# Decode values of a paged attention: four samples on GpSimd with a buffer and load requests of its own, four on TensorE

## The reference

```python
k_past = cache_k[l][page_table].reshape(b_s, n_past, FOX_H, FOX_HD)   # 8 samples x 1024 x 4 x 128
v_past = cache_v[l][page_table].reshape(b_s, n_past, FOX_H, FOX_HD)
...
p = jax.nn.softmax(jnp.concatenate([s_past, s_new], axis=-1), axis=-1)
o = einsum('bhqk,bkhd->bqhd', p[..., :P], v_past) + einsum('bhqk,bkhd->bqhd', p[..., P:], v)
```

## Time and profile before

| | |
|---|---|
| median of 3 runs | 1726.88 us (1726.18 to 1727.52) |
| the profiled execution | 1725.65 us |
| its span | 1723.9 us |
| TensorE busy | 1699.3 us (99%) |
| VectorE busy | 1077.7 us (63%) |
| ScalarE busy | 798.8 us (46%) |
| GpSimd busy | 142.4 us (8%) |

### The profile page before, as it was taken

One profiled execution on the slowest core, in us unless ns is written; L12 is line 12 of the kernel. 1 busy time (PEld: TensorE's weight loads), 2 busy tenths in 40 slices (PEclk: granted clock), 3 DMA queues, 4 the chain that ended last, 5 costly groups with the idle time before them and its releaser, 6 DMA issues.

```text
span 1723.9 us, 33330 instructions
## 1 busy us (share of the span) xinstructions
PE 1699.3 (99%) x13788; PEld 1648.4 (96%) x13788; DVE 1077.7 (63%) x1263; ACT 798.8 (46%) x895; POOL 142.4 (8%) x148
## 2 busy tenths in 40 slices
PE   9999999999999999999999999999999999999995
PEld 8999888899999999999999999999999999999995
DVE  7888787756557666455587784444444444454655
ACT  5654544556544444444454554444444444333433
POOL 8200000000012555000000000000000000000000
PEclk9999999999999999999999999999999999999998
DMA  8565567776657877666555556555555555555651
GB/s 263 150 209 159 148 203 245 225 235 209 213 153 238 282 252 250 189 179 183 179 176 183 173 170 192 178 180 181 182 179 178 180 182 182 181 178 169 194 175 73
DMA packets 309126, 329.75 MB, mean 191 GB/s; under 512 B 12175, under 2 KB 289939, under 8 KB 308756
## 3 DMA queue, kind: packets, MB, share of 16 engines
q1 hardware_dynamic: 307612, 326.59, 61.7%
q10 hardware_dynamic: 1400, 1.54, 0.2%
HBM read 322.31 MB, written 5.77 MB: 190 GB/s over the span
## 4 chain that ended last, share of the span: by engine, by line
PE 96%; DVE 2%; DMA 1%; issue 0%; ACT 0%; ACTq 0%; SPq 0%; DVEq 0%
PE ps L778 15%; PE ps L779 15%; PE ps L1155 15%; PE ps L1156 15%; PE ps L780 15%; PE ps L1154 15%; PE ps L848 1%; PE ps L1027 1%; DMA w_in_ring<-in_w_in 1%; PE ps L827 0%; PE ps L883 0%; PE ps L816 0%; PE ps L801 0%; DVE w_split L1624 0%; PE ps L794 0%
## 5 line engine op out<-in xcount | busy, mean ns | idle before, releaser
L2310 DVE TENSOR_TENSOR w_lo<-w_raw,w_hi 128x1024 fp32r<-128x1024 f32 x264 | 322.8, 1225 | 326.0 <-ACT w_hi L1512 323.0
L1624 DVE TENSOR_TENSOR w_split<-w_in_ring,w_split 128x1024 fp32r<-128x1024 f32 x276 | 352.6, 1283 | 238.7 <-ACT w_split L1216 229.0
L778 PE MATMUL ps<-xh,w_split 128*128 128x264 f32 x1680 | 482.2, 287 | 1.7 <-DVE w_split L1624 1.7
L1512 ACT ACTIVATE w_hi<-w_raw 128x1024 fp32r<-128x1024 f32 x264 | 279.4, 1060 | 440.0 <-PE ps L1156 435.2
L779 PE MATMUL ps<-xl,w_split 128*128 128x264 f32 x1680 | 478.2, 285 | 0.0
L780 PE MATMUL ps<-xh,w_split 128*128 128x264 f32 x1680 | 476.7, 284 | 0.0
L1216 ACT ACTIVATE w_split<-w_in_ring 128x1024 fp32r<-128x1024 f32 x276 | 291.1, 1059 | 361.7 <-DMA w_in_ring<-in_w_in 268.1
L778 PEld LDWEIGHTS ps<-xh,w_split 128*128 128x128 f32 x1680 | 316.0, 188 | 20.2 <-issue 14.6
L1155 PE MATMUL ps<-x1l,w_hi 128*128 128x264 f32 x1152 | 327.8, 285 | 0.0
L1156 PE MATMUL ps<-x1h,w_lo 128*128 128x264 f32 x1152 | 327.0, 284 | 0.0
L1154 PE MATMUL ps<-x1h,w_hi 128*128 128x264 f32 x1152 | 326.0, 283 | 0.0
(11 more groups left out here) (473 smaller groups left out, 2138.8 us busy)
## 6 DMA issues: line engine op xcount, KB each, us to landing
w_in_ring<-in_w_in SPq DMA_DIRECT2D x210, 512.0 KB, 3.8
w_raw<-in_w_ffn_up SPq DMA_DIRECT2D x176, 512.0 KB, 3.5
w_raw<-in_w_ffn_down SPq DMA_DIRECT2D x88, 512.0 KB, 3.4
kv<-in_cache_k SPq DMA_DIRECT2D x64, 258.0 KB, 3.8
w_in_ring<-in_w_branch SPq DMA_DIRECT2D x32, 512.0 KB, 4.3
kv<-in_cache_v SPq DMA_DIRECT2D x64, 256.0 KB, 3.8
w_in_ring<-in_w_out SPq DMA_DIRECT2D x32, 512.0 KB, 3.4
x_t<-in_x SPq DMA_DIRECT2D x8, 264.0 KB, 6.6
```

The source lines that it names most:

```text
L778: nc.tensor.matmul(out, w_split[:, slot, 0, c], right_h[:, k, :], start=first, stop=False)
L1512: A_(w_hi[:, n % RING2, :], raw[:, n % RING2, :], ACT.Copy).then_inc(sem("hi2"), 1)
L1624: V.tensor_tensor(w_split[:, slot, 1, :], w_in_ring[:, slot, 1, :], w_split[:, slot, 0, :], ALU.subtract).then_inc(sem("lo_done"), 1)
L2310: V.tensor_tensor(w_lo[:, n % RING2, :], raw[:, n % RING2, :], w_hi[:, n % RING2, :], ALU.subtract).then_inc(sem("lo2"), 1)
```

## The change

GpSimd takes samples 0 to 3 whole (`V_POOL` = 4), and TensorE samples 4 to 7, in eight units at chunks `V_AT` = 155, 162, 168, ... 200. Buffer 0 of `kv` serves TensorE's units, loaded by SyncE; buffer 1 serves GpSimd. Its first four pages are loaded by SyncE behind chunk 154; for all later ones GpSimd loads the page number into a register and issues the DMA itself, for each page as soon as it has added it. GpSimd waits for each page by a semaphore of its own, and before it first writes the rows 2 and 3 of `v_sum` for the last chunk of branch 1. `v_add` is called once, ahead of TensorE's last unit, with four sums. The places of all other work stay.

```diff
-V_AT = [155 + 3 * u for u in range(16)]
-V_SCALED = [1, 3, 5, 7, 9, 11, 13]
+V_POOL = 4
+V_AT = [155, 162, 168, 175, 181, 188, 194, 200]
...
         def load_values(u, first):
-            if first == 0 and u < 2:
-                sp.wait_ge(sem("kv_used"), 16 + u - 1)
-                sp.wait_ge(sem("lf_taken"), 16 + u - 1)
-            elif first == 0 and u - 2 in V_SCALED:
-                sp.wait_ge(sem("v_scaled"), V_SCALED.index(u - 2) + 1)
-            elif first == 0:
-                sp.wait_ge(sem("kv_used"), 16 + len([v for v in range(u - 1) if v not in V_SCALED]))
-            pages("cache_v", u, first, u // 2, MIX)
+            if first == 0 and u == 0:
+                sp.wait_ge(sem("lf_taken"), 15)
+            if first == 0:
+                sp.wait_ge(sem("kv_used"), 16 + u if u else 15)
+            for j in (first, first + 1):
+                src = A["cache_v"][ds(page_register(8 * (V_POOL + u // 2) + 4 * (u % 2) + j), 1)].rearrange("o p c -> (o p) c")
+                sp.dma_start(kv[:, 0, j, 0:MIX], src).then_inc(sem("kv0"), 16)
+
+        def load_pool_values():
+
+            sp.wait_ge(sem("kv_used"), 16)
+            sp.wait_ge(sem("lf_taken"), 16)
+            for j in range(4):
+                src = A["cache_v"][ds(page_register(j), 1)].rearrange("o p c -> (o p) c")
+                sp.dma_start(kv[:, 1, j, 0:MIX], src).then_inc(sem("kv1"), 16)
...
+            if n == 154:
+                load_pool_values()
+            for u in range(8):
+                for first in (0, 2):
+                    if n == (V_AT[u - 1] + 6 if u else 152) + first // 2:
+                        load_values(u, first)
...
+        pool.wait_ge(sem("pt_loaded"), 16)
+        pool.wait_ge(*told("f_ptt", 1))
+        for u in range(2 * V_POOL):
+
+            b, half = u // 2, u % 2
+            out = v_sum[:, b, :]
+            if u == 4:
+
+                pool.wait_ge(*used(last_chunk(pass_of("branch", 1, 7))))
             for j in range(4):
-                at = 32 * (8 * b + 4 + j) + b
-                values = kv[:, u % 2, j, 0:MIX]
-                scaled = out if j == 0 else values
+                at = 32 * (8 * b + 4 * half + j) + b
+                values = kv[:, 1, j, 0:MIX]
+                first = half == 0 and j == 0
+                scaled = out if first else values
+                if u:
+                    pool.wait_ge(sem(f"kv_page{j}"), 16 * u)
+                elif j == 0:
+                    pool.wait_ge(sem("kv1"), 64 * 9)
                 then(pool.tensor_tensor(scaled.rearrange("p (h d) -> p h d", h=HEADS), values.rearrange("p (h d) -> p h d", h=HEADS),
                                         ptt[:, at:at + HEADS * DEC].rearrange("p (h m) -> p h m", m=DEC)[:, :, 0:1].to_broadcast([P, HEADS, P]),
                                         ALU.mult))
-                if j:
+                if not first:
                     then(pool.tensor_tensor(out, out, values, ALU.add))
-            pool.sem_inc(sem("v_scaled"), 1)
+                if u < 2 * V_POOL - 1:
+                    page = pool.value_load(pt[0:1, 4 * (u + 1) + j:4 * (u + 1) + j + 1], min_val=0, max_val=A["cache_v"].shape[0] - 1)
+                    pool.dma_start(values, A["cache_v"][ds(page, 1)].rearrange("o p c -> (o p) c")).then_inc(sem(f"kv_page{j}"), 16)
+        pool.sem_inc(sem("v_scaled"), 1)
...
+            b, half = V_POOL + u // 2, u % 2
             bank = claim(pe, "v_unit", 0)[0] if u == 0 else banks("v_unit", 0)[0]
-            if u == 8:
-                v_add(0, 4)
-            if u == 15:
-                v_add(4, 7)
-            pe.wait_ge(sem(f"kv{u % 2}"), 64 * (8 + u // 2 + 1))
+            if u == 7:
+                v_add()
+            pe.wait_ge(sem("kv0"), 64 * (8 + u + 1))
```

## The result

The changed kernel takes 1728.24 us (median of 20 runs, 1726.52 to 1729.61), beside 1725.35 for the kernel before in as many runs on the same chip (1724.11 to 1727.52). The ratio is 1.0013, with a 95% interval of 1.0007 to 1.0019. The difference of the medians is 2.9 us. The interval lies above 1: the change makes the kernel slower by about 0.1 to 0.2%, where 2.05 us faster was forecast. That is a small difference, within the 0.2% that the prediction would still have called the same, but on the wrong side of zero. The time lies in the range of 1723.2 to 1733. The forecast of 1724.8 was reckoned from 1726.88, the median of three runs; from 1725.35 it would have been 1723.3, so the sum is off by 4.9 us. The profiled execution took 1729.45 us, of which 1727.8 are its span.

The account below looks back on a forecast made before the run. TensorE's own instructions were taken to bound the kernel (96% of the chain); one unit (1.20) and three additions (0.85) fewer give 1725.65 - 2.05 = 1723.6, plus 1.23 for the median, 1724.8 us. Range: 1723.2 to 1733.

Parts of the forecast that it names:

- TensorE's part: On TensorE between chunks: one value unit (1.20 us) and three additions (0.85) fewer, 2.05 us less on the path.
- GpSimd's part: GpSimd's arithmetic 102.7 us plus 28 page loads 49.3, from 537.0 to 689.0, 7.0 us before TensorE needs the sum.
- GpSimd late: Rival, chance 0.27: page loads cost more than 1.76 us, TensorE waits ahead of its last unit; 1725 to 1751 us.
- SyncE and the loads: SyncE issues 36 value pages instead of 64, no longer waits for GpSimd (19.1 us before); nothing new waits, counted as nothing.
- Chunk 155: Four pages at chunk 154 delay chunk 155's weight load by some 2 us; 4.5 us of slack take it.
- VectorE, the term that turned the sign: GpSimd's added arithmetic delays VectorE's splits 3.2 us more over 150, hidden by VectorE's 49.6 us of waits nearly everywhere.
- the stall: TensorE's wait for VectorE's w_split at 581.72, kept at 1.15 us; that it goes or shrinks had chance 0.10.
- VectorE falls behind: Rival, chance 0.10: five more collisions with GpSimd in 551.4 to 568.6, stalls of 2 to 5 us, 1727 to 1730.
- requests held up by VectorE: Skill page's ground for the GpSimd late rival (0.27): GpSimd can't write DMA requests while VectorE is in two-port mode.

Follow-up runs that it names:

- e8: Kernel before the change, with fills in place of GpSimd's arithmetic: 1723.53 us, ratio 0.9984 to the kernel before.
- e6: Changed kernel with GpSimd's first pages in pairs behind chunks 146 and 147, and fills for its arithmetic: 1722.35 us, ratio 0.9983 to the kernel before.
- e4: Changed kernel with first pages in pairs behind chunks 146 and 147, and GpSimd pausing ahead of its eighth page until VectorE's cum_rows: 1722.1 us, ratio 0.9985.
- e3: Changed kernel without GpSimd's 28 page loads and their waits, working eight times on its first four pages: 1729.17 us, ratio 1.0024 to the kernel before.
- e2: Changed kernel with fills in place of GpSimd's multiplications and additions, page loads kept: 1722.56 us, ratio 0.9983 to the kernel before.
- e7: Changed kernel with first pages in pairs behind chunks 146 and 147, and GpSimd pausing ahead of its 17th page until chunk 178 is used: 1726.75 us, ratio 1.0003.
- e1: Changed kernel with GpSimd's first four pages loaded in two pairs behind chunks 146 and 147, not all behind chunk 154: 1726.4 us, ratio 1.0001.
- e5: Changed kernel with only GpSimd's pause ahead of its eighth page until VectorE's cum_rows: 1724.95 us, ratio 0.9993 to the kernel before.

## Why the prediction went wrong

The matmuls at both ends of the stretch give the account. These are the ends in the kernel before; then in the changed kernel; in e8; in e6 (TensorE's timelines):

```profile
546.07 1.07 PE L883 MATMUL ps<-kv,ptt 128*32 128x512 f32 x8
...
705.95 0.51 PE L893 MATMUL ps<-fold,v_part 128*128 128x8 f32 x4
```
```profile
546.37 1.07 PE L897 MATMUL ps<-kv,ptt 128*32 128x512 f32 x8
...
709.29 0.51 PE L907 MATMUL ps<-fold,v_part 128*128 128x8 f32 x4
```
```profile
546.23 0.64 PE L880 MATMUL ps<-kv,ptt 128*32 128x512 f32 x4
...
704.16 0.39 PE L890 MATMUL ps<-fold,v_part 128*128 128x8 f32 x3
```
```profile
546.19 0.64 PE L894 MATMUL ps<-kv,ptt 128*32 128x512 f32 x4
...
702.06 0.95 PE L904 MATMUL ps<-fold,v_part 128*128 128x8 f32 x8
```

| stretch, us | GpSimd's arithmetic | fills | lost to the arithmetic |
| --- | --- | --- | --- |
| before | 159.88 | 157.93 | 1.95 |
| changed | 162.92 | 155.87 (e6) | 7.05 |
| difference | +3.04 | -2.06 | +5.10 |

- **TensorE's part, right in the stretch.** A unit and three additions were put at 2.05 us; without collisions they are 2.06, by one trace each. e4 does the real work and has 155.87 too. Over the whole kernel no such gain is shown: e8 and e6 have ratios of 0.9984 and 0.9983.
- **GpSimd's part, right in the sum, partly by luck.** These are its third page load with the work on the page behind it, and its last addition, from its timeline in the changed kernel:

```profile
554.36 0.58 POOL L761 DMA_DIRECT2D kv<-in_cache_v  x1 [1.20 <-issue]
554.96 1.06 POOL L754 TENSOR_TENSOR kv<-kv,ptt 128x512 f32<-128x512 f32 x1
556.09 2.19 POOL L758 TENSOR_TENSOR v_sum<-v_sum,kv 128x512 f32<-128x512 f32 x1
...
685.17 2.15 POOL L758 TENSOR_TENSOR v_sum<-v_sum,kv 128x512 f32<-128x512 f32 x1
```

  A page costs 1.20 + 0.58 and the gap of 0.02, 1.80, beside 1.76 foreseen. The split was the other way about: the issue 0.58 where 1.05 was taken, the steps ahead of it 1.20 where SyncE's 0.71 was. GpSimd ends at 687.3 (689.0 foreseen), though it began at 540.90 and not at 537.0: it needed 146.4 us and not 152.0, and the two errors cancel. TensorE asks for the sum at 701.5, so 14 us lie between (6.7 in e4, where TensorE has no stalls). The rival with the largest chance, GpSimd late, fell; e3, in which it ends at 650, says the same from the other side.
- **SyncE and the loads, right but for one.** Its waits for GpSimd are gone, and no load of a value page made TensorE wait.
- **Chunk 155, the first step that failed.** It was said that the four pages hold its load back by some 2 us and that 4.5 us of slack take it. It went out at 532.9, 2.4 us later than before, and ScalarE split it 3.8 us later (539.02 against 535.21 before). What the step missed is that the split and ptt stand in line on ScalarE, and that VectorE's last two reciprocals of lnt stand behind the splits. VectorE's last reciprocal in the kernel before, and in the changed kernel:

```profile
542.36 1.79 DVE L2231 RECIPROCAL lnt<-lnt 128x264 f32<-128x264 f32 x1
```
```profile
546.79 1.79 DVE L2245 RECIPROCAL lnt<-lnt 128x264 f32<-128x264 f32 x1
```

  So VectorE went into its run of wide products 4.4 us late. Of these, 2.95 are the late load (chunk 155's split begins at 540.18 and not at 537.23). The other 1.5 are collisions with GpSimd, which starts at 540.90: two instructions between have their long forms, 1.55 for 0.70 and 2.00 for 1.37; in e2, with fills, the last reciprocal is back at 544.2. TensorE didn't feel chunk 155 itself; the slack that hid it was the slack that the next term needed.
- **VectorE, the term that turned the sign.** Its delay was scaled by GpSimd's busy time: 3.2 us more over 150, and the stall kept at 1.15. The rows say otherwise. Here are GpSimd's groups in 530 to 720 and then VectorE's splits in 540 to 700 of the changed kernel, beside the earlier trace rows:

```profile
L758 POOL TENSOR_TENSOR v_sum<-v_sum,kv 128x512 f32<-128x512 f32 x28 | 54.6, 1950 | 2.2
L754 POOL TENSOR_TENSOR kv<-kv,ptt 128x512 f32<-128x512 f32 x28 | 33.3, 1188 | 0.8
L761 POOL DMA_DIRECT2D kv<-in_cache_v x28 | 16.4, 585 | 34.5 <-issue 34.5
L754 POOL TENSOR_TENSOR v_sum<-kv,ptt 128x512 f32<-128x512 f32 x4 | 4.7, 1163 | 30.2 <-ACTq L245 30.1
```
```profile
L1638 DVE TENSOR_TENSOR w_split<-w_in_ring,w_split 128x1024 fp32r<-128x1024 f32 x48 | 80.0, 1681 | 35.9 <-ACT w_split L1230 33.8
```

  GpSimd's shortest multiplication is 1.05 and its shortest addition 1.28. Above these it lost (43.2 - 29.4) + (36.4 - 26.9) = 23.3 us before and (38.0 - 33.6) + (54.6 - 35.8) = 23.2 after: eleven more instructions, and no more delay. VectorE, against the busy time with fills, lost 108.25 - 87.94 = 20.3 before and 124.56 - 89.86 = 34.7 after. So all the new delay fell on VectorE, 14.4 us. The prediction reckoned with the splits alone: 3.2 us more, where they took 48 x (1.681 - 1.225) = 21.9 us beyond the short form, 8.0 more than before. The multiplications, now behind a page issue, got short (1.54 to 1.19); the additions got longer (1.74 to 1.95). That VectorE lost more is measured. The pause of the issue can be a part of the cause only: in e3, without issues, GpSimd loses (52.9 - 33.6) + (52.2 - 35.8) = 35.7 us, 12.5 more, and VectorE 120.6 - 89.9 = 30.7, 4 less, which is still 10 more than in the kernel before.

  The place was wrong too. It was said that bl and the split are in their long form already, so that the stall can hardly grow. VectorE's timeline in the changed kernel:

```profile
554.77 2.37 DVE L2249 TENSOR_TENSOR hf<-hf,lnt 128x1056 f32<-128x1056 f32 x1
...
562.30 2.18 DVE L1638 TENSOR_TENSOR w_split<-w_in_ring,w_split 128x1024 fp32r<-128x1024 f32 x1
...
585.43 2.25 DVE L2273 SCALAR_TENSOR_TENSOR cum_k<-cum,ident 4x1024 fp32r<-4x1024 f32 x1
```

  The first product ran in 1.25 us before and takes 2.37; the split at 562.30 ends at 564.48, and TensorE, waiting for it since 562.60, goes on at 564.62. The stall of 581.72 didn't grow where it was but shrank (0.41 at 583.97); two others opened on either side, 19 us ahead and 5 us behind. A long form at one place said nothing on its neighbours.
- **The rival "VectorE falls behind" named the mechanism** (collisions in 551 to 569, a slack of 4.5 us, 1727 to 1730) and got 0.10. What spoke for it, five more collisions against 4.5, was in the text; what was set against it was 2.24 us of idle time ahead of 568.28. The late chunk 155 takes 3 us from that same slack. Two terms drew on one account and each was checked against it alone; together, 2 to 3 and 5 against 4.5, they should have made it the likeliest case.
- **The clock wasn't in the sum.** 1.7 of the 5.1 us come from 3.4 us at 1.2 GHz. The traces with 3.4 us or more of waits in this stretch have such a drop at 589 or 590.5 (the changed kernel, e3, e7); those with at most 2.04 (before, e1, e2, e4, e5, e6, e8) have none there. But waits alone don't settle it. All ten traces have a single wait of 2.0 to 2.2 us for w_lo at 923 to 932; behind it the clock falls for 3.4 us in three of them (before, changed, e8) and not in the other seven. Here are the kernel before, then e4, the wait and the window behind it:

```profile
927.19 0.36 PE L1154 MATMUL ps<-zh,w_hi 128*128 128x266 f32 x1 [2.01 <-DVE w_lo L2310]
...
927.00:933.00 6.00, 5.81 (x35) 5.84 (x36) 5.57 (x10) 2.73 (x5) 0.00 (x0) 0.72 0.69 200
```
```profile
923.47 0.36 PE L1170 MATMUL ps<-zh,w_hi 128*128 128x266 f32 x1 [2.02 <-DVE w_lo L2326]
...
923.00:929.00 6.00, 5.53 (x44) 5.56 (x45) 5.57 (x10) 2.73 (x5) 0.00 (x0) 1.00 0.64 187
```

  Such drops are also most of what sets one execution apart from another. In the 66 executions of the kernel before that were timed beside the experiments, the mean granted clock was 0.996 in 22, 0.995 in 29 and 0.994 in 15, and their mean times are 1724.5, 1726.0 and 1727.5: steps of 1.5 us, about the price of one drop. So the 1.7 us in the stretch are what one traced execution lost; how often the changed kernel loses them there isn't known. The waits have 3.25 of the 5.1 us, 4.4 less 1.15. What is left, 7.05 - 4.4 - 1.7 = 1.0, no row names, but the kernel before has as much, 1.95 - 1.15 = 0.8, so it hardly enters the difference.
- **Outside the stretch,** the span grew by 3.9 us in all against 3.04 in it: 0.3 lies ahead of unit 0, 0.6 behind the fold. One part of that is plain: the wait for ml, 0.6 before and 1.1 after (0.9 to 1.4 in e1, e2 and e4 to e7). So a part of TensorE's gain is given back later: e8 and e6 are 2.06 apart in the stretch and 2.4 in their spans, but 1.7 of these are the drop of the clock that only e8 has at 926, and their ratios are the same within their intervals.
- **The range held by luck.** It was drawn wide for a GpSimd that is late; 1728.24 lies in it for another reason.

The section Who interferes with whom of the Trainium skill's page "SBUF — State Buffer" says that a VectorE instruction with two inputs in SBUF contends with a GpSimd instruction that reads SBUF and not with one that only writes. The runs agree: 1225 ns a split beside fills (e2), 1681 beside arithmetic. The rival that the same section suggested, requests held up by VectorE, wasn't seen: the 28 issues on GpSimd took 577 ns in the middle and 776 at most.

## What to carry to other kernels

Work moved from the bounding engine to an idle one is paid for by whoever shares a resource with the idle one; price it where the third engine's queue has the least slack, not over the stretch, and add up all terms that draw on the same slack before holding them against it. A measured mean of two engines' mutual delay need not scale with busy time: here GpSimd's share stayed and VectorE's grew by 70%, and without the issues the shares were different again. Where the spot is known, let the helper engine stand aside for just that long: 6.5 us of pause and an earlier load turned 0.13% slower into 0.15% faster, and GpSimd was still done 6.7 us ahead of need. And differences of 0.1% are of the size of one drop of the clock, so they want many runs, and the trace of more than one execution.

## What the runs showed of the hardware

- A page load issued by GpSimd with its page number from a register keeps GpSimd for 0.58 us, and 1.20 us of steps stand ahead of it; on SyncE the two together are 1.07.
- When GpSimd's arithmetic and VectorE's two-input products overlap, who is held up isn't fixed: with eleven more instructions GpSimd lost 23.2 us as before (23.3), VectorE 34.7 in place of 20.3; without page issues between them (e3) GpSimd lost 35.7 and VectorE 30.7. With fills GpSimd was busy for 62.8 (e8) to 93.3 us (e2) of 540 to 700, and VectorE's splits took 1225 ns throughout.
- TensorE's granted clock fell to the lower level for 3.4 us, a loss of 1.7 us, after three waits that came to 4.4 us between 562.6 and 589.1. After a single wait of some 2 us at 923 to 932 it fell in three traces and didn't in seven; the times of the kernel before lie in steps of 1.5 us by the mean granted clock (0.996, 0.995, 0.994).
